# Expert sums of the second layer's sample rows built channel by channel, with their closing norm in that layout

## The chip, the cores and the metric

The kernel runs on one core of a Trainium2 chip. The metric is the device time of one execution in microseconds. Three runs of the kernel before gave 2985.22, 2985.74 and 2985.90 us, median 2985.74 us.

## The reference, cut to what matters

One inference step of a two-layer decoder: 512 prompt tokens and 8 sample tokens, 1024 channels, float32. Each layer has a mixer (attention and convolution in the first, pooling in the second) and then the part that fills most of the time, a retrieval of experts:

```python
def peer_ffn(h, wq, subkeys, u_tab, v_tab):
    ...
    expert = i1 * N_KEYS + i2                  # 16 of 16384 experts for each token and head
    g = jax.nn.softmax(cs, axis=-1)
    act = gelu(einsum('nd,nhkd->nhk', h, u_tab[expert]))
    return einsum('nhk,nhkd->nd', g * act, v_tab[expert])
...
xs = xs + peer_ffn(rms_norm(xs, norm_ffn[l]), ...)
y_prompt = rms_norm(xp, norm_final)
y_sample = rms_norm(xs, norm_final)
```

For each token and each of 8 heads, 16 experts are picked. Each brings a row u (1024 values, for a dot with the token) and a row v (1024 values, which is added with the weight of the dot). A closing RMS norm makes the two outputs y_prompt and y_sample.

## The kernel before

A **task** is one head of one tile of 128 prompt tokens: 16 steps, and in each step GpSimd gathers for each of the 128 tokens the pair (u, v) of one expert, 8 KB for each partition, 1 MB in all, into one of 8 slots of the buffer RING (line 935). A layer has 4 tiles of 8 heads, 32 tasks, and then one task for the 8 samples, in which the 128 partitions hold 64 (head, sample) pairs twice over, so that 8 steps (`PAIRS`) do for all of them. That sample task of the second layer is the last of the kernel, task 65.

What a step goes through, engine by engine:

- VectorE multiplies the u half of the slot with the token rows and sums it to a dot (`product`, line 2039; a row of one custom instruction and one read of the accumulator).
- ScalarE makes the gelu (L1500), the weight times it (`gate`, L1505) and a matrix `diag` (L1509): the identity times the weight for a prompt tile (128x128), the selector `sel_b` times it for the samples (128x8, which adds up the 16 partitions of each sample).
- TensorE multiplies (`accumulate`, line 1308): `diag` is the stationary operand, the v half of the slot the moving one, in two halves of 512 columns, into two PSUM banks. The sum of a tile stays in PSUM through its steps. Its end frees the slot (`v_freed`), for which GpSimd waits before it gathers the eighth step after.

In the trace a float32 matmul of the program shows as two records, each with its own weight load.

After the last step of a tile VectorE adds the sum to the rows X (`add_unit`, line 2070). The closing norm has three parts: `squares` (VectorE, lines 1566 and 1571), `root` (ScalarE, line 1410), `normed_rows` (VectorE, lines 1577 and 1585). The table `CLOSING` says at which step of which task they are issued; for the last prompt tile they are put into the sample task, `root` at step place 9 and `normed` at place 12 (in the sample task a step has two places: step 4 has places 8 and 9, step 6 has 12 and 13, step 7 has 14 and 15). For the samples they follow after everything else: `add_unit`, `squares`, `root`, `normed_rows`, then the store by the SP queue (line 727).

Beside the steps, the rest of the work of the next half-layer (projections, attention, pooling, query and key scores) is cut into **pieces**. `pieces` lists them with a weight each and `agenda` spreads them over the steps in proportion to the weights; each engine issues its part of a piece behind its part of that step. For the second half of the second layer the query pieces `q` lie between steps 704 and 816. `jobs_of` gives each piece its use of one of the PSUM banks that the pieces share in turn.

## Time and profile before

| | |
|---|---|
| median of 3 runs | 2985.74 us |
| the profiled execution | 2987.37 us, span of its trace 2985.4 us |
| granted TensorE clock, mean over the span | 0.972 |
| TensorE / VectorE / ScalarE / GpSimd busy | 87% / 70% / 43% / 41% |
| gathers by GpSimd | 1040 of 1 MB |
| mean rate of the DMA engines | 406 GB/s |
| the last gather | issued at 2959.33 us |

The trace's times are counted from the start of the span. The end of the span is the landing of the last store, y_sample. A granted clock of 1.00 is TensorE's upper level (2.4 GHz), 0.50 the lower (1.2 GHz); values between are means over a stretch in which it changed.

### The profile page before, as it was taken

The numbers are of one execution on the slowest core, as the hardware profiler recorded it, in microseconds if no ns is written. First come the engines' busy times: TensorE is split into PE (matmuls) and PEld (weight loads), VectorE is DVE, ScalarE is ACT, GpSimd is POOL, SyncE is SP. The second block draws the span as 40 slices with busy tenths as digits, with TensorE's granted clock in tenths as the row PEclk, the third lists the DMA queues.
The fourth block names the chain that finished last, engine by engine and source line by source line (L and its number), as shares of the span: only waits on it lengthen the run. The fifth ranks groups of instructions, "written<-read, shape, count | busy, mean of one in ns | idle before, by whom it ended". The sixth has DMA issues, their size and how long they took to land.

```text
span 2985.4 us, 26394 instructions
## 1 busy us (share of the span) xinstructions
PE 2590.8 (87%) x7285; PEld 1273.1 (43%) x7285; DVE 2076.5 (70%) x4938; ACT 1281.4 (43%) x3753; POOL 1220.2 (41%) x1104
## 2 busy tenths in 40 slices
PE   8999998999988888888888888888999978777787
PEld 6675564555544443334444334333444422222222
DVE  2657766887767667776667677777666766677666
ACT  2113445555434435444444444445443444444444
POOL 2013543444444434444444444445334444444442
PEclk9999999999999999999999999999999999999999
DMA  9979999999999999999999999999999999999997
GB/s 354 353 276 388 396 421 415 422 398 406 421 421 421 421 421 394 421 420 421 422 421 421 411 409 410 421 421 419 417 421 420 409 422 411 421 417 418 407 415 330
DMA packets 174565, 1213.29 MB, mean 406 GB/s; under 512 B 19685, under 2 KB 20721, under 8 KB 32843
## 3 DMA queue, kind: packets, MB, share of 16 engines
q0 software_dynamic: 155904, 1124.11, 91.5%
q1 hardware_dynamic: 18515, 87.51, 7.5%
q8 instruction: 58, 0.95, 0.1%
q14 instruction: 88, 0.72, 0.1%
HBM read 1206.90 MB, written 38.37 MB: 417 GB/s over the span
## 4 chain that ended last, share of the span: by engine, by line
DMA 45%; PE 36%; DVE 8%; ACT 6%; issue 3%; POOL 1%; ACTq 0%; POOLq 0%; DVEq 0%
DMA RING<-in_peer_uv,idx 44%; PE PSUM L1308 22%; PE PSUM L987 10%; DVE RING L2039 4%; ACT diag L1509 2%; ACT L1500 1%; PE PSUM L998 1%; ACT gate L1505 1%; DMA RING<-in_peer_uv,pidx 1%; POOL RING L935 1%; PE PSUM L969 1%; ACT act_h L1500 1%; ACT L1488 1%; PE PSUM L1296 1%; PE PSUM L1086 0%
## 5 line engine op out<-in xcount | busy, mean ns | idle before, releaser
L1308 PE MATMUL PSUM<-RING,diag 128*128 128x512 f32 (+1 forms) x4032 | 1957.3, 622 | 359.6 <-ACT diag L1509 353.3
L935 POOL DMA_INDIRECT RING<-in_peer_uv,idx x1024 | 1168.5, 1141 | 1550.3 <-PE PSUM L1308 1426.8
L2039 DVE CUSTOM_DVE_ANT_0 RING<-RING,H 128x1024 f32<-128x1024 f32 x1032 | 1262.3, 1224 | 703.3 <-DMA RING<-in_peer_uv,idx 697.5
L1308 PEld LDWEIGHTS PSUM<-RING,diag 128*128 128x128 f32 (+1 forms) x4032 | 731.5, 193 | 1425.7 <-ACT diag L1509 788.7
L1500 ACT ACTIVATE act_h<-dots 128x1 f32<-128x1 f32 x1040 | 208.1, 200 | 1108.7 <-DVE dots L2039 1107.1
L1509 ACT ACTIVATE diag<-ident,gate 128x128 f32<-128x128 f32 x992 | 398.3, 402 | 33.1 <-PE PSUM L1308 0.6
L987 PE MATMUL PSUM<-HT,WCH 128*128 128x256 f32 (+2 forms) x1408 | 334.0, 384 | 1.4 <-ACT HT L1361 1.3
L1505 ACT ACTIVATE gate<-act_h,ex 128x1 f32<-128x1 f32 x992 | 292.1, 294 | 32.3
L987 PEld LDWEIGHTS PSUM<-HT,WCH 128*128 128x128 f32 x1408 | 265.1, 192 | 93.6 <-issue 61.7
L1500 ACT ACT_TABLE_LOAD x90 | 115.5, 1283 | 5.6 <-DVE dots L2039 4.0
L1361 ACT ACTIVATE YT<-PSUM 128x256 f32<-128x256 f32 (+4 forms) x70 | 27.3, 390 | 173.9 <-PE PSUM L987 157.4
L2039 DVE DVE_READ_ACCUMULATOR2_ANT dots<- 128x1 f32 x1040 | 85.3, 82 | 0.0
L1488 ACT ACT_TABLE_LOAD x66 | 84.7, 1283 | 1.2
L1380 ACT ACTIVATE H<-H,negm 128x128 f32<-128x128 f32 (+3 forms) x32 | 18.0, 562 | 98.7 <-DVE negm L1741 98.6
L1296 PEld LDWEIGHTS PSUM<-SKT,YT 128*128 128x128 f32 (+1 forms) x316 | 41.4, 172 | 34.2 <-issue 29.9
L969 PE MATMUL PSUM<-ident,H 128*128 128x128 f32 (+1 forms) x200 | 33.9, 290 | 18.0 <-POOL POOL_STATE_M L884 9.7
L1296 PE MATMUL PSUM<-SKT,YT 128*128 128x128 f32 (+1 forms) x316 | 49.2, 278 | 0.0
L924 POOL DMA_DIRECT2D out_win_v_sample<-in_state_win_v x16 | 9.8, 617 | 92.9 <-PE PSUM L987 59.9
L987 PE MATMUL PSUM<-HT,RING 128*128 128x264 f32 x192 | 46.9, 402 | 0.0
L2017 DVE TENSOR_TENSOR onehot<-cij,iota 128x512 f32<-128x512 uint32 x65 | 44.6, 687 | 0.0
L2020 DVE TENSOR_TENSOR onehot<-onehot,si 128x512 f32<-128x512 f32 x65 | 44.6, 685 | 0.0
L2022 DVE TENSOR_REDUCE picked<-onehot 128x32 f32<-128x512 f32 x65 | 44.2, 680 | 0.0
(265 smaller groups left out, 1535.4 us busy)
## 6 DMA issues: line engine op xcount, KB each, us to landing
WCH<-in_peer_wq SPq DMA_DIRECT2D x28, 1024.0 KB, 9.1
WCH<-in_w_in_ab SPq DMA_DIRECT2D x18, 1024.0 KB, 9.6
RING<-in_peer_uv,idx POOLq DMA_INDIRECT x1024, 15.0
out_win_k_sample<-in_state_win_k POOLq DMA_DIRECT2D x8, 2016.0 KB, 12.0
out_win_v_sample<-in_state_win_v POOLq DMA_DIRECT2D x8, 2016.0 KB, 11.0
RING<-in_w_in_ab SPq DMA_DIRECT2D x6, 1024.0 KB, 11.8
WCH<-in_w_out_ab SPq DMA_DIRECT2D x6, 1024.0 KB, 9.6
X<-in_x_prompt SPq DMA_DIRECT2D x4, 512.0 KB, 4.4
```

The costliest lines, as they stand in the source:

```text
L935: pool.indirect_dma_start(rows[:, use % SLOTS, :], None, peer_uv.rearrange("l e n -> (l e) n"), bass.IndirectOffsetOnAxis(ap=at, axis=0),) ...
L969: last = nc.tensor.transpose(out[0:cols, n * width:n * width + rows], src, ident[0:rows, 0:rows])
L987: last = nc.tensor.matmul(out[:, lo:width], w[k], rows[:, k, lo:width], start=(k == 0), stop=(k == KD - 1))
L1296: last = nc.tensor.matmul(out[0:m, j * P:(j + 1) * P], qp[:, hc % 2, j * P:j * P + m], SKT[:, hc, :], start=True, stop=True)
L1308: last = nc.tensor.matmul(PSUM[0:out_n, accumulator(n) + half, :], diag[:, at % DIAGS, 0:out_n], rows[:, use % SLOTS, D + half * 512:D + h ...
L1488: nc.scalar.activation(ex[:, par, :], cs[:, par, :], ACT.Exp, bias=ncs[:, par:par + 1], accum_out=exsum[:, par:par + 1]).then_inc(gates_ex ...
L1500: chain(nc.scalar.activation(act_h[:, st, column], dots[:, st, column], ACT.Gelu))
L1505: chain(nc.scalar.activation(gate[:, st, column], act_h[:, st, column], ACT.Copy, scale=weight))
L1509: nc.scalar.activation(diag[:, at % DIAGS, 0:n], selector, ACT.Copy, scale=gate[:, st, column]).then_inc(diag_ready, 1)
L2017: left(V.tensor_tensor(onehot[:], cij[:].unsqueeze(3).to_broadcast([P, 2, TOP, TOP]), iota16[:].unsqueeze(1).unsqueeze(1).to_broadcast([P, ...
L2020: left(V.tensor_tensor(onehot[:], onehot[:], si[:].unsqueeze(2).to_broadcast([P, 2, TOP, TOP]), ALU.mult))
L2039: V.tensor_tensor_reduce(out=u, in0=u, in1=row, scale=1.0, scalar=0.0, op0=ALU.mult, op1=ALU.add, accum_out=dots[:, tau % SETS, k:k + 1]). ...
```

## The change

Three things are edited.

1. **The sum of the last task.** In the second layer's sample task `accumulate_turned` takes the place of `accumulate`. The roles of the operands are exchanged: the v half of the slot is the stationary operand, in 8 pieces of 128 channels, and `diag` (128x8) the moving one. So a step has 8 matmuls with 8 columns each in place of 2 with 512, and the sum stands with channels on the partitions: 128 x (8 pieces x 8 samples), in one PSUM bank. The residual is put in ahead of the first step by one matmul with the identity.
2. **The closing norm of the samples**, `last_unit`, in that layout: copy out of PSUM, square, a matmul with a matrix of 1/1024 that sums the squares over the partitions (`last_mean`), the product with the gains, a sum over the 8 pieces, root, reciprocal, product; all on 128x64 values or less. The store writes 128 rows of 64 values, and the host turns them round. For it the residual rows and the gains are needed in the new layout: a new piece `turned` (weight 1.5, at key column 8 of the queries of the last half-layer) has 16 small transposes on TensorE, two copies by ScalarE, and a memset by VectorE. The buffer is COUNT, which has no reader by then.
3. **The last tile's norm**: `normed` moves from place 12 to place 14 of the sample task, behind the dot of step 7. `root` stays at place 9.

```diff
-NORMS = (..., (1,), (2,), (3,), (4,), (0,))
+NORMS = (..., (1,), (2,), (3,), (4,))
...
+        if hc == 8 and (l, b) == (1, 1):
+            out.append((("turned",), 1.5))
...
-        found[task + 3 * (t == 0), 4 if t == 0 else 12] = [("normed", FINAL + t, 0)]
+        found[task + 3 * (t == 0), {0: 4, T - 1: 14}.get(t, 12)] = [("normed", FINAL + t, 0)]
...
-            sp.wait_ge(rows_normed, rows_by(FINAL + T))
-            store(y_sample.rearrange("b s d -> (b s) d"), Hv[0:B, 0, :])
+            sp.wait_ge(last_normed, 1)
+            store(y_sample, last_y)
...
+                if kind == "turned":
+                    pe.wait_ge(rows_normed, rows_by(FINAL - 1))
+                    for half in range(2):
+                        wait_emptied(pe, ("gain", FINAL, half))
+                    out = open_bank(piece)
+                    for c in range(KD):
+                        nc.tensor.transpose(out[:, c * B:(c + 1) * B], X[0:B, 0, c * P:(c + 1) * P], ident[0:B, 0:B])
+                    for c in range(KD):
+                        last = nc.tensor.transpose(out[:, KD * B + c:KD * B + c + 1], G[0:1, c * P:(c + 1) * P], ident[0:1, 0:1])
+                    close_bank(last, piece)
...
+            def accumulate_turned(n, tau, k):
+
+                use = first(tau) + k
+                at = tensor_rows(use)
+                out = PSUM[:, accumulator(n), 0:KD * B]
+                if k == 0:
+                    wait_emptied(pe, ("turned",))
+                    nc.tensor.matmul(out, ident[:], last_x, start=True, stop=False, skip_group_check=True)
+                pe.wait_ge(diag_ready, at + 1)
+                for c in range(KD):
+                    last = nc.tensor.matmul(out[:, c * B:(c + 1) * B], rows[:, use % SLOTS, D + c * P:D + (c + 1) * P],
+                                            diag[:, at % DIAGS, 0:B], start=False, stop=k == steps(tau) - 1,
+                                            skip_group_check=True)
+                last.then_inc(v_freed, 1)
+
+            def last_mean(n):
+
+                pe.wait_ge(mean_ready, 1)
+                pe.wait_ge(last_squared, 1)
+                nc.tensor.matmul(PSUM[:, accumulator(n) + 1, 0:KD * B], mean, last_square,
+                                 start=True, stop=True).then_inc(last_summed, 1)
...
-                    accumulate(n, sample_task(l), k, B, True, True)
+                    if l == L - 1:
+                        accumulate_turned(n, sample_task(l), k)
+                    else:
+                        accumulate(n, sample_task(l), k, B, True, True)
...
+                if kind == "turned":
+                    wait_full(act, piece)
+                    nc.scalar.activation(last_x, bank(piece)[:, 0:KD * B], ACT.Copy)
+                    emptied(nc.scalar.activation(last_g, bank(piece)[:, KD * B:KD * B + KD], ACT.Copy), piece)
...
-            front(("root", FINAL + T))
+            act.wait_ge(last_reduced, 1)
+            nc.scalar.activation(last_root, last_root, ACT.Sqrt, bias=eps[:, 0:1]).then_inc(last_rooted, 1)
...
+                dve.wait_ge(v_freed, tensor_rows(first(tau) + steps(tau)))
+                step(V.tensor_copy(last_y, total))
+                V.tensor_tensor(last_square, last_y, last_y, ALU.mult).then_inc(last_squared, 1)
+                wait_emptied(dve, ("turned",))
...
+                dve.wait_ge(last_summed, 1)
+                V.tensor_reduce(last_root, PSUM[:, accumulator(n) + 1, 0:KD * B].rearrange("p (c b) -> p b c", c=KD),
+                                AX.X, ALU.add).then_inc(last_reduced, 1)
+                dve.wait_ge(last_rooted, 1)
+                step(V.reciprocal(last_root, last_root))
...
-            add_unit(unit(1, T))
-            dve.wait_ge(acc_added, unit(1, T + 1))
-            squares(FINAL + T, 0)
-            normed_rows(FINAL + T, 0)
+            last_unit()
```

The first place is the end of TensorE's order. The last rows before (L1308 is the sum; 452 matmuls of the last prompt tiles, then the samples' 16):

```order
L1296 MATMUL PSUM<-SKT,YT 128x128 x2
L1296 MATMUL PSUM<-SKT,YT 8x128
L1308 MATMUL PSUM<-RING,diag 128x512 x452
L1308 MATMUL PSUM<-RING,diag 8x512 x16
L425 UNCONDITIONAL_BRANCH
```

And of the change (L1333 is the sum, L1346 to L1349 the new one, L1358 the mean of the squares):

```order
L1321 MATMUL PSUM<-SKT,YT 128x128 x2
L1321 MATMUL PSUM<-SKT,YT 8x128
L1333 MATMUL PSUM<-RING,diag 128x512 x452
L1346 MATMUL PSUM<-COUNT,ident 128x64
L1349 MATMUL PSUM<-diag,RING 128x8 x64
L1358 MATMUL PSUM<-COUNT 128x64
L429 UNCONDITIONAL_BRANCH
```

16 matmuls whose output is 8x512 have become 64 whose output is 128x8, with one ahead of them and one behind.

The second place is the end of VectorE's order. Before (L2039 is the dot, L1577 and L1585 the norm, L2070 the addition of the sum to X, L1566 and L1571 the squares):

```order
L2039 ISA dots 128x1
L1577 RECIPROCAL rstd<-rstd 128x5
L1585 SCALAR_TENSOR_TENSOR H<-X,rstd,G 128x1024
L2039 ISA RING,dots<-RING,KT 128x1024
L2039 ISA dots 128x1
L2070 TENSOR_TENSOR X<-PSUM,X 8x512 x2
L1566 ISA H,ss<-X 8x1024
L1566 ISA ss 8x1
L1571 TENSOR_SCALAR ss<-ss 128x5
L1577 RECIPROCAL rstd<-rstd 128x5
L1585 SCALAR_TENSOR_TENSOR H<-X,rstd,G 8x1024
```

Of the change (L2097 is the dot, L1633 and L1641 the norm of the last tile, L2138 and below `last_unit`):

```order
L2097 ISA RING,dots<-RING,KT 128x1024
L2097 ISA dots 128x1
L1633 RECIPROCAL rstd<-rstd 128x5
L1641 SCALAR_TENSOR_TENSOR H<-X,rstd,G 128x1024
L2138 COPY COUNT<-PSUM 128x64
L2139 TENSOR_TENSOR COUNT<-COUNT 128x64
L2141 TENSOR_TENSOR COUNT<-COUNT 128x64
L2144 TENSOR_REDUCE COUNT<-PSUM 128x8
L2147 RECIPROCAL COUNT<-COUNT 128x8
L2148 TENSOR_TENSOR COUNT<-COUNT 128x64
```

The norm of the last tile stands behind the last dot, and six instructions on 64 values or fewer for each partition have taken the place of six on 1024 or 512.

The third place is TensorE's order around the new piece, of the change (L1002 are query projections, L1321 key scores):

```order
L1321 MATMUL PSUM<-SKT,YT 128x128 x2
L1321 MATMUL PSUM<-SKT,YT 8x128
L1333 MATMUL PSUM<-RING,diag 128x512 x2
L1285 MATMUL PSUM<-ident,X 128x8 x8
L1287 MATMUL PSUM<-ident,G 128x1 x8
L1333 MATMUL PSUM<-RING,diag 128x512 x6
L1002 MATMUL PSUM<-HT,WCH 128x264 x4
```

The 16 transposes (L1285, L1287) stand in one lump between two steps; the query pieces after them lie up to 5 steps later than before, those ahead of them up to 3 steps earlier, and the last of them where they lay.

## Rows read from the trace of the kernel before

**Rows 1.** The page: shares of the chain that ended last, by engine.

```profile
DMA 45%; PE 36%; DVE 8%; ACT 6%; issue 3%; POOL 1%; ACTq 0%; POOLq 0%; DVEq 0%
```

**Rows 2.** Timeline of the last 30 us: start us, us, engine line op, xcount [idle before].

```profile
2959.74 1.88 PE L1308 MATMUL PSUM<-RING,diag 128*8 128x512 f32 x4 [0.69 <-ACT diag L1509]
...
2967.21 1.22 DVE L2039 CUSTOM_DVE_ANT_0 RING<-RING,KT 128x1024 f32<-128x1024 f32 x1 [1.25 <-DMA RING<-in_peer_uv,pidx]
...
2970.88 1.28 ACT L1500 ACT_TABLE_LOAD   x1
...
2972.04 1.22 DVE L2039 CUSTOM_DVE_ANT_0 RING<-RING,KT 128x1024 f32<-128x1024 f32 x1 [1.12 <-DMA RING<-in_peer_uv,pidx]
...
2973.09 5.58 PE L1308 MATMUL PSUM<-RING,diag 128*8 128x512 f32 x12 [1.81 <-ACT diag L1509]
...
2974.61 1.22 DVE L2039 CUSTOM_DVE_ANT_0 RING<-RING,KT 128x1024 f32<-128x1024 f32 x1
...
2976.44 0.30 ACT L1509 ACTIVATE diag<-sel_b,gate 128x8 f32<-128x8 f32 x1
...
2978.71 1.28 DVE L2070 TENSOR_TENSOR X<-PSUM,X 8x512 f32<-8x512 f32 x2 [2.87 <-PE PSUM L1308]
...
2981.48 0.21 ACT L1410 ACTIVATE rstd<-ss 128x5 f32<-128x5 f32 x1 [3.44 <-DVE ss L1571]
...
2983.25 0.30 SPq L727 DMA_DIRECT2D out_y_sample<-H  x1
```

**Rows 3.** DMA engines' GB/s in 40 slices of 0.1 us, 2972 to 2976 us.

```profile
GB/s 0 82 0 0 82 0 0 82 0 0 0 82 0 0 82 0 0 82 0 0 0 0 0 0 0 0 0 0 0 0 0 0 0 0 0 287 328 492 451 328
```

**Rows 4.** TensorE's timeline, behind an idle time (last row), and 16 narrow matmuls of the pooled samples.

```profile
1802.52 0.38 PE L1116 MATMUL PSUM<-POOL_NEW_M,H 8*128 8x8 f32 x2
...
1806.95 0.59 PE L1116 MATMUL PSUM<-POOL_NEW_M,H 8*128 8x8 f32 x2
...
2928.84 10.55 PE L1308 MATMUL PSUM<-RING,diag 128*128 128x512 f32 x20 [2.10 <-ACT diag L1509]
```

**Rows 5.** Stretches: us, busy PE, PEld, DVE, ACT, POOL, then granted clock, DMA share, GB/s.

```profile
1803.00:1804.00 1.00, 1.00 (x8) 0.94 (x8) 0.83 (x1) 0.00 (x0) 0.68 (x1) 1.00 1.04 434
1807.00:1808.00 1.00, 1.00 (x4) 0.94 (x4) 0.72 (x2) 0.39 (x3) 0.00 (x0) 0.50 1.06 442
...
161.50:162.00 0.50, 0.50 (x4) 0.47 (x3) 0.00 (x0) 0.00 (x0) 0.00 (x0) 0.74 0.97 406
162.00:162.50 0.50, 0.50 (x3) 0.47 (x3) 0.00 (x0) 0.00 (x0) 0.00 (x0) 0.50 1.10 406
...
2930.00:2931.00 1.00, 1.00 (x2) 0.33 (x1) 1.00 (x1) 0.00 (x0) 0.00 (x0) 0.50 1.08 451
```

**Rows 6.** Timeline, 8 narrow matmuls of the attention's samples.

```profile
159.94 0.38 PE L1046 MATMUL PSUM<-ident,RING 8*128 8x8 f32 x2
...
161.85 0.59 PE L1046 MATMUL PSUM<-ident,RING 8*128 8x8 f32 x2
...
162.37 0.59 PE L1047 MATMUL PSUM<-RING 64*128 64x8 f32 x2
162.99 0.19 DVE L1829 COPY YT<-PSUM 128x32 f32<-128x32 f32 x1 [3.69 <-PE PSUM L1047]
```

**Rows 7.** Timeline behind the pooled samples: a gather's issue and two dots.

```profile
1811.15 1.52 POOL L935 DMA_INDIRECT RING<-in_peer_uv,idx  x1 [7.47 <-PE PSUM L1308]
...
1818.03 1.24 DVE L2039 CUSTOM_DVE_ANT_0 RING<-RING,H 128x1024 f32<-128x1024 f32 x1 [0.63 <-DMA RING<-in_peer_uv,idx]
...
1820.83 1.23 DVE L2039 CUSTOM_DVE_ANT_0 RING<-RING,H 128x1024 f32<-128x1024 f32 x1 [0.95 <-DMA RING<-in_peer_uv,idx]
```

**Rows 8.** Stretches where the new piece will lie, and the end of the queries.

```profile
2260.00:2280.00 20.00, 19.63 (x62) 10.16 (x61) 13.41 (x30) 10.41 (x30) 8.81 (x9) 1.00 1.01 419
2375.00:2380.00 5.00, 5.00 (x16) 2.83 (x16) 3.92 (x14) 2.67 (x10) 3.06 (x3) 1.00 0.95 343
```

**Rows 9.** A small copy out of PSUM: ns min/median/max.

```profile
L1681 DVE COPY RING<-PSUM x1: 225/225/225, 31.6 to 31.6; 128x64 f32<-128x64 f32 x1
```

More of the change, by code:

```diff
@@ L81 @@
 TASKS = T * PH + 1
-NORMS = ((1, 2, 0), (1, 2, 0), (3, 4), (3, 4), (1, 2), (1, 2), (3, 4, 0), (3, 4, 0), (1,), (2,), (3,), (4,), (0,))
+NORMS = ((1, 2, 0), (1, 2, 0), (3, 4), (3, 4), (1, 2), (1, 2), (3, 4, 0), (3, 4, 0), (1,), (2,), (3,), (4,))
 FINAL = 8
@@ L371, in jobs_of @@
         return [(kind, piece[1], half) for half in range(2)]
+    if kind == "turned":
+        return [piece]
     if kind == "scored_sample":
@@ L496, in build @@
         rows = RING[:, :].rearrange("p (s n) -> p s n", n=ROW)
+        mean = COUNT[:, 0, :]
+        last_y, last_square = (COUNT[:, 1, n * KD * B:(n + 1) * KD * B] for n in range(2))
+        last_x = COUNT[:, 2, 0:KD * B]
+        last_g = COUNT[:, 2, KD * B:KD * B + KD]
+        last_root = COUNT[:, 2, KD * B + KD:KD * B + KD + B]
         hrep = (H[:, BT * D + D:BT * D + 2 * D], KT[:, :, :].rearrange("p c n -> p (c n)")[:, 0:D])
@@ L651, in build @@
         acc_added = sem("acc_added")
+        mean_ready = sem("mean_ready")
+        last_squared = sem("last_squared")
+        last_summed = sem("last_summed")
+        last_reduced = sem("last_reduced")
+        last_rooted = sem("last_rooted")
+        last_normed = sem("last_normed")
         def bank(name):
@@ L1344, in _ @@
                 for k in range(PAIRS):
-                    accumulate(n, sample_task(l), k, B, True, True)
+                    if l == L - 1:
+                        accumulate_turned(n, sample_task(l), k)
+                    else:
+                        accumulate(n, sample_task(l), k, B, True, True)
                     front_at(sample_task(l), k)
+            last_mean(unit(L - 1, T))
             assert len(opened) == len(JOBS)
@@ L1461, in front @@
                     copy_out(piece, pT_s[:, :, :], wide(piece, KD, B))
+                if kind == "turned":
+                    wait_full(act, piece)
+                    nc.scalar.activation(last_x, bank(piece)[:, 0:KD * B], ACT.Copy)
+                    emptied(nc.scalar.activation(last_g, bank(piece)[:, KD * B:KD * B + KD], ACT.Copy), piece)
                 if kind == "gain":
@@ L1912, in front @@
                     counted(*piece[1:])
+                if kind == "turned":
+                    V.memset(mean, 1.0 / D).then_inc(mean_ready, 1)
                 if kind == "qrep":
@@ L2073, in _, with last_unit @@
             NT = 2 * NK
+            def last_unit():
+                n, tau = unit(L - 1, T), sample_task(L - 1)
+                total = PSUM[:, accumulator(n), 0:KD * B]
+                dve.wait_ge(v_freed, tensor_rows(first(tau) + steps(tau)))
+                step(V.tensor_copy(last_y, total))
+                V.tensor_tensor(last_square, last_y, last_y, ALU.mult).then_inc(last_squared, 1)
+                wait_emptied(dve, ("turned",))
+                step(V.tensor_tensor(last_y.rearrange("p (c b) -> p c b", c=KD), last_y.rearrange("p (c b) -> p c b", c=KD),
+                                     last_g.unsqueeze(2).to_broadcast([P, KD, B]), ALU.mult))
+                dve.wait_ge(last_summed, 1)
[3 more added lines that the diff above has]
+                step(V.reciprocal(last_root, last_root))
+                V.tensor_tensor(last_y.rearrange("p (c b) -> p c b", c=KD), last_y.rearrange("p (c b) -> p c b", c=KD),
+                                last_root.unsqueeze(1).to_broadcast([P, KD, B]), ALU.mult).then_inc(last_normed, 1)
             def search_step(at):
@@ L2154 @@
         "norm_final"]
-_OUTS = [("y_prompt", (1, SEQ, D)), ("y_sample", (B, 1, D)), ("conv_prompt", (1, 1, 2, DA)),
+_OUTS = [("y_prompt", (1, SEQ, D)), ("y_sample", (P, KD * B)), ("conv_prompt", (1, 1, 2, DA)),
          ("conv_sample", (1, B, 2, DA)), ("win_k_prompt", (1, SEQ, DA)), ("win_k_sample", (1, B, PAST, DA)),
@@ L2187 @@
     out = {name: r.results[0][f"out_{name}"] for name, _ in _OUTS}
+    out["y_sample"] = _np.ascontiguousarray(out["y_sample"].reshape(P, KD, B).transpose(2, 1, 0)).reshape(B, 1, D)
     for name in ("win_k_prompt", "win_v_prompt"):
```

## The prediction

> **What bounds the kernel now.** I read the shares of the chain that ended last first [rows 1]: the landings of the gathers have 45% of it, TensorE 36%. That is the long middle, which the change touches in one place. The rest of the change lies in the last 26 us, so the timeline of that stretch decides [rows 2]. The reader is to see two halves in it. Until 2974.6 us VectorE waits for landings: step 3's dot starts at 2967.21 with 1.25 us of waiting and step 6's at 2972.04, also behind a wait, so a step lands every 2.4 to 2.5 us. Behind that stands a serial tail. The last `diag` is ready at 2976.74 (2976.44 + 0.30); TensorE works on steps 5, 6 and 7 without a pause from 2973.09 to 2978.67, 1.86 us a step. It is late there because ScalarE, which had made the last tile's root, had to load the gelu's table again at 2970.88. Then addition, squares, root and norm of the samples follow one another from 2978.71 to the store at 2983.25, 4.54 us, and 2.15 us later the span ends.
>
> **The change, part by part.**
>
> *The norm of the last tile.* It moves behind step 7's dot. Before, that dot began at 2974.61, behind the norm. When had its row landed? The DMA engines' slices show one 8 KB packet about every 0.33 us, the last at 2973.7 [rows 3], and step 6, whose row ended eight packets earlier, started its dot some 0.7 us behind its own last packet. So step 7 could have started at about 2974.45: the move gives 0.15 us, and only where TensorE is not behind. I take 0; the two ends are 0 and 0.15. The norm itself runs while TensorE sums, and its store, issued near 2977.2, lands long before the end.
>
> *The closing norm of the samples.* Removed are 4.54 us. Added behind TensorE's last matmul: a copy of 128x64 out of PSUM, 0.23 [rows 9]; a square, about 0.2 (nearest is the same row); the mean matmul with 64 columns, 0.4 at full clock (a narrow one alone takes 0.38 [rows 4]), 0.65 at half (0.59 [rows 6], and more columns); the sum over 8 pieces, the reciprocal and the last product, about 0.2 each (rows 9 again is nearest); the root, 0.21 [rows 2]; handovers between the engines, 0.03 to 0.05 each, 0.2. The gains' product lies beside the mean matmul. The sum is 1.85 us at full and 2.1 us at half clock, in place of 4.54: 2.4 to 2.7 us saved. The table for the root is loaded while TensorE still works, as before. The store moves the same 32 KB in 128 short pieces instead of 8 long ones; no row shows that price, I leave 2.15 us, with 0 and +0.5 as ends.
>
> *The sum of the last task.* A step becomes 8 matmuls with 8 moving columns and a new 128-column stationary operand each. The same shape is in the trace: in the pooled samples, 14 matmuls begin from 1802.52 to 1806.95, 0.316 us each [rows 4]. So a step costs 8 x 0.316 = 2.53 us instead of 1.86, 20.2 us for the task. The Trainium skill ("TensorE: Matmul & The Clock Gate", "LDWEIGHTS" and "Back-to-back issue gap") gives 107 ns for a load of 128 columns and 25 ns for a small matmul; from it I estimate 16 x 132 ns = 2.1 us a step, which would fit between two landings and take about 1.2 us off the full-clock sum below. The row goes first, and it says that TensorE is as slow as the landings already at full clock. At full clock, then: step 5's `diag` comes at 2973.05 as before, 24 matmuls follow, TensorE ends at 2973.09 + 7.58 = 2980.7 instead of 2978.7; + 1.85 + 2.15 = 2984.7. That alone is 0.7 us better than 2985.4.
>
> *But the clock will not stay.* Both places in the trace where TensorE does nothing but such narrow matmuls lose it. In the pooled samples it is 1.00 at 1803 and 0.50 from 1807 on, though TensorE was busy all the time [rows 5]; in the attention's samples, which start at 159.94, it falls within 161.5 to 162.0 and stands at 0.50 at 162.0 [rows 5, 6]. So the clock goes from its upper level (2.4 GHz) to its lower (1.2 GHz) 1.8 to 4.7 us into such a stream. It falls 40 times in the whole span; in all others TensorE had just stood idle, as the 2.10 us before 2928.84 and the 0.50 at 2930 show [rows 4, 5]. There the wide matmuls that follow bring it back; in the last task nothing wide follows. At the lower level the matmuls begin 0.52 us apart (161.85 to 162.37 [rows 6]), and VectorE gets the result at 162.99; I take 0.525. The 64 matmuls start at 2959.74 [rows 2]; the one ahead of them fits into TensorE's wait of 0.69 us there. With the fall 4.4 us in (nearer the second case, since here wide matmuls go before as there), 14 run at 0.316 (4.4 us) and 50 at 0.525 (26.3 us): TensorE ends at 2990.4, 11.8 us later than before. The landings are over by then; no `diag` is waited for any more (step 5's is ready at 2973.05, when TensorE would be at step 3). + 2.1 + 2.15 = 2994.7. The ends: a fall after 1.8 us, 2.0 us more; 0.45 to 0.60 for a matmul, 3.8 us to either side.
>
> *The piece `turned`.* 16 narrow matmuls, 16 x 0.316 = 5.1 us on TensorE at step 765, near 2270 us, with VectorE's memset and two copies by ScalarE of 0.2 us each, which nobody waits for. TensorE frees the slots of the ring, so this holds up the gathers. The pooled samples are the same lump: the next gather was issued after 7.47 us of waiting, and yet the dots slipped only from 2.48 to 2.80 us apart at one place [rows 7], 0.3 to 0.4 us in all, because eight slots were under way. At the new place TensorE is fuller, 19.63 of 20 us [rows 8]. I take 0.7 us. Upper end: nothing hidden, 5.1 + 1.7 for a fallen clock = 6.8; lower end: the pieces' shift removes the dip of 343 GB/s at 2375 [rows 8], which costs (421 - 343)/421 x 5 = 0.9 us.
>
> **The sum.** 2994.7 + 0.7 = 2995.4 against a span of 2985.4: +10.0 us. The profiled execution took 2987.37 us, so it would take 2997.4; it lies 1.6 us above the median of the runs, to which I add the same 10.0 (with rounding 10.1): **2995.8 us**, 0.34% slower. What a measurement of this kernel can tell from no change is 0.2%, 6.0 us.
>
> **The rivals.**
>
> *A: the clock stays up.* Then the span is 2984.7 + 0.7 = 2985.4, no change, 2985.7 us. The point from which it decides: every microsecond that the fall comes later is worth 0.66 us, and with no fall before 2979 there is nothing lost. For it speaks that TensorE would work without a gap from 2959.7 on, and 38 of 40 falls follow gaps; against it the two streams of rows 5 and 6, of which one was busy without a gap as well. The Trainium skill's rule is that the clock is lost where TensorE idles between bursts (the same page, "HAM oscillation — how this bites in real kernels"); by that rule a gapless stream keeps it and rival A holds. The trace disagrees at 1807. 14%.
>
> *B: TensorE at 0.5 is slower still.* If a narrow matmul doubles with the clock, 0.63, then 50 x 0.105 = 5.3 us more: 3001 us. Against: 161.85 to 162.37. 5%.
>
> *C: the lump hits the ring.* TensorE is over 90% busy there and the next pieces follow at once; if 3 to 5 us come through beside the forecast: 2999 to 3001 us. Against: rows 7. 7%.
>
> *D: the new sum costs nothing.* If a narrow step takes no more than the 1.86 us of a wide one and the clock stays, TensorE ends at 2978.7 as before, and 1.85 + 2.15 + 0.7 behind it make a span of 2983.4, 2983.7 us by the median. Against: rows 4. 3%.
>
> **How the numbers follow.** The forecast, a fall within 5 us and 0.5 to 0.56 a matmul, has 71%: 2992 to 2998. B and C lie above, A and D below. The range 2989.5 to 3000.5 holds the forecast, most of C and the lower end of the narrow matmuls' price; A, D and most of B are left out, just under 2 in 10. Slower by over 0.2% (above 2991.7): forecast, B, C, less 3% for a late fall or a cheap matmul, 0.80. Faster by over 0.2% (below 2979.8): no case reaches it, 0.01. Within: 0.19.
>
> **What would show it.** The granted clock at 0.50 from about 2964 us to the end; TensorE busy without a gap from 2959.7 to 2990; matmuls of L1349 0.32 us apart first, 0.52 later; VectorE's copy (L2138) waiting over 10 us for TensorE; from it to the store 2.1 us; the root's table loaded long before. Around 2270 us a wait of GpSimd for TensorE of 6 to 8 us, the clock at 0.50 for some microseconds, the dots late by under 1 us. The forecast is wrong if the clock stays at 1.00 in the last 20 us, if the last task's matmuls run in less than 0.25 us, or if the rows after 2300 us are shifted by more than 3 us against before.

## The result and the profile after

| | before | after |
|---|---|---|
| median of 22 runs each | 2985.43 us (2982.72 to 2989.22) | 2989.64 us (2985.62 to 2994.12) |
| profiled execution | 2987.37 us | 2986.24 us |
| its span | 2985.4 us | 2984.3 us |
| mean granted clock of TensorE | 0.972 | 0.966 |

The ratio is 1.0014, 95% interval 1.0008 to 1.0020: the change costs 4.2 us. That is real and small, under the 0.2% (6.0 us) that the prediction called no change. The forecast was 2995.8 us, 10.1 us more: the sign and the mechanism were right, the size was more than twice what came, and the result lies only 0.1 us inside the lower end of the range (2989.5). That it lies inside is luck, since the interval of the ratio alone spans 2.4 to 6.0 us over the kernel before. The class on which I put 0.80, slower by over 0.2%, did not come.

The profiled execution of after is shorter than that of before, though its median is longer. The middle ends some microseconds earlier or later from run to run (here the last task starts at 2954.53, before at 2959.74 [rows 2]), so spans of single executions don't compare. What compares is **the tail**: from TensorE's first matmul of the last task to the end of the span. Before it is 2985.4 - 2959.74 = 25.7 us, after 2984.3 - 2954.53 = 29.8 us: +4.1 us, as much as the medians differ. The medians leave nothing for the middle, within the 2 us either way that their interval leaves open; the trace of the middle, below, shows no loss there either.

TensorE's timeline of the changed kernel's end (start us, us, engine line op, xcount in matmul records, of which a float32 matmul makes two, and the idle time before):

```profile
2951.95 1.98 PE L1333 MATMUL PSUM<-RING,diag 128*128 128x512 f32 x4 [0.50 <-ACT diag L1564]
2953.77 0.33 PE L1346 MATMUL PSUM<-COUNT,ident 128*128 128x64 f32 x2
2954.53 1.95 PE L1349 MATMUL PSUM<-diag,RING 128*128 128x8 f32 x16 [0.43 <-ACT diag L1564]
2956.82 2.26 PE L1349 MATMUL PSUM<-diag,RING 128*128 128x8 f32 x16 [0.34 <-ACT diag L1564]
2959.29 20.65 PE L1349 MATMUL PSUM<-diag,RING 128*128 128x8 f32 x96 [0.21 <-ACT diag L1564]
2980.61 0.66 PE L1358 MATMUL PSUM<-COUNT 128*128 128x64 f32 x2 [0.67 <-DVE COUNT L2139]
```

Step 0 takes 1.95 us and TensorE then waits for the next `diag`: at full clock a narrow step is hardly dearer than a wide one (1.88 [rows 2]), and the landings set the pace as before. Step 1 already takes 2.26. From step 2 on six steps run without a gap in 20.65 us, 3.44 us each, and TensorE is the bound. The stretches say why (us, busy PE, PEld, DVE, ACT, POOL, granted clock, DMA share, GB/s):

```profile
2956.00:2958.00 2.00, 1.67 (x16) 1.57 (x15) 1.96 (x3) 0.70 (x3) 0.00 (x0) 1.00 1.01 422
2958.00:2959.00 1.00, 1.00 (x7) 0.98 (x7) 0.34 (x2) 0.56 (x3) 0.00 (x0) 0.65 1.05 434
...
2960.00:2970.00 10.00, 10.00 (x49) 10.00 (x49) 6.27 (x12) 5.97 (x15) 0.00 (x0) 0.50 0.37 155
2970.00:2979.00 9.00, 9.00 (x44) 9.00 (x44) 2.10 (x4) 2.08 (x4) 0.00 (x0) 0.50 0.14 58
```

The granted clock falls in the stretch 2958 to 2959; 0.65 there is 30% at 1.00 and 70% at 0.50, so at about 2958.3, 3.8 us into the narrow stream. It stands at 0.50 (1.2 GHz) to the end, with TensorE busy all the time.

The other engines at the end (same columns; lines not of TensorE left in):

```profile
2967.02 1.22 DVE L2097 CUSTOM_DVE_ANT_0 RING<-RING,KT 128x1024 f32<-128x1024 f32 x1 [1.21 <-DMA RING<-in_peer_uv,pidx]
...
2969.48 1.23 DVE L2097 CUSTOM_DVE_ANT_0 RING<-RING,KT 128x1024 f32<-128x1024 f32 x1 [1.23 <-DMA RING<-in_peer_uv,pidx]
...
2979.98 0.23 DVE L2138 COPY COUNT<-PSUM 128x64 f32<-128x64 f32 x1 [7.84 <-PE PSUM L1349]
...
2981.37 0.23 DVE L2144 TENSOR_REDUCE COUNT<-PSUM 128x8 f32<-128x64 f32 x1 [0.78 <-PE PSUM L1358]
2981.63 0.30 ACT L1588 ACTIVATE COUNT<-COUNT,eps 128x8 f32<-128x8 f32 x1 [8.72 <-DVE COUNT L2144]
...
2982.45 0.33 SPq L742 DMA_DIRECT2D out_y_sample<-COUNT  x1
```

Step 7's dot (2969.48) waits for its landing, 2.46 us behind step 6's: with the norm out of the way VectorE is at the landings' pace. It did not matter, since TensorE began step 7 only near 2976.5 (one step of 3.44 us before its end), 5 us behind the `diag` of that step (made at 2971.61). VectorE waits 7.84 us for TensorE's last sum. From its copy to the store's issue are 2.47 us instead of 4.54 (2978.71 to 2983.25 [rows 2]), from the issue to the end 1.85 instead of 2.15.

The piece `turned`, in the middle, from TensorE's part of the timeline:

```profile
2255.15 0.65 PE L1285 MATMUL PSUM<-ident,X 8*128 8x8 f32 x8
...
2255.67 0.63 PE L1287 MATMUL PSUM<-ident,G 1*128 1x1 f32 x8
...
2256.22 1.98 PE L1333 MATMUL PSUM<-RING,diag 128*128 128x512 f32 x4
```

16 transposes are 16 records, not 32: a float32 transpose shows as one record here, a float32 matmul as two. The lump takes 1.07 us (2255.15 to 2256.22), and the clock stays at 1.00 there. VectorE's dots around it start at 2253.24, 2255.72, 2258.26 and 2260.70, still 2.4 to 2.5 us apart, and GpSimd's waits for TensorE next to it are 1.45 and 2.05 us. So two signs that the prediction gave did not come, a wait of GpSimd of 6 to 8 us and some microseconds at 0.50.

### The profile page after: what moved, and what is told of

The parts are those of the page before. It is cut to its first block, busy times and chain, and to the rows that moved or that the text cites. A ratio compares the mean times of both kernels' runs of the same rounds, so it can differ in the third digit from the quotient of the medians.

```text
span 2984.3 us, 26630 instructions
## 1 busy us (share of the span) xinstructions
PE 2599.8 (87%) x7401; PEld 1298.7 (44%) x7401; DVE 2073.6 (69%) x4938; ACT 1281.4 (43%) x3755; POOL 1233.7 (41%) x1104
## 4 chain that ended last, share of the span: by engine, by line
DMA 46%; PE 36%; DVE 8%; ACT 7%; issue 3%; POOL 1%; ACTq 0%; POOLq 0%; DVEq 0%
DMA RING<-in_peer_uv,idx 44%; PE PSUM L1333 21%; PE PSUM L1002 9%; DVE RING L2097 4%; ACT diag L1564 2%; ACT L1555 1%; ACT gate L1560 1%; DMA RING<-in_peer_uv,pidx 1%; PE PSUM L1013 1%; ACT act_h L1555 1%; PE PSUM L984 1%; PE PSUM L1349 1%; ACT L1543 1%; POOL RING L950 1%; PE PSUM L1321 1%
## 5 line engine op out<-in xcount | busy, mean ns | idle before, releaser
L1333 PE MATMUL PSUM<-RING,diag 128*128 128x512 f32 x4000 | 1940.1, 622 | 351.3 <-ACT diag L1564 345.6
L950 POOL DMA_INDIRECT RING<-in_peer_uv,idx x1024 | 1183.6, 1156 | 1532.5 <-PE PSUM L1333 1401.7
L2097 DVE CUSTOM_DVE_ANT_0 RING<-RING,H 128x1024 f32<-128x1024 f32 x1032 | 1262.6, 1224 | 695.6 <-DMA RING<-in_peer_uv,idx 689.5
L1333 PEld LDWEIGHTS PSUM<-RING,diag 128*128 128x128 f32 x4000 | 730.2, 194 | 1398.4 <-ACT diag L1564 766.1
L1002 PE MATMUL PSUM<-HT,WCH 128*128 128x256 f32 (+2 forms) x1408 | 334.2, 384 | 1.6 <-ACT HT L1412 1.4
L1002 PEld LDWEIGHTS PSUM<-HT,WCH 128*128 128x128 f32 x1408 | 265.4, 192 | 94.1 <-issue 62.1
L2097 DVE DVE_READ_ACCUMULATOR2_ANT dots<- 128x1 f32 x1040 | 85.9, 83 | 0.0
L1321 PEld LDWEIGHTS PSUM<-SKT,YT 128*128 128x128 f32 (+1 forms) x316 | 42.0, 174 | 34.5 <-issue 30.2
L1321 PE MATMUL PSUM<-SKT,YT 128*128 128x128 f32 (+1 forms) x316 | 49.7, 280 | 0.0
L1002 PE MATMUL PSUM<-HT,RING 128*128 128x264 f32 x192 | 46.9, 402 | 0.0
## 6 DMA issues: line engine op xcount, KB each, us to landing
RING<-in_w_in_ab SPq DMA_DIRECT2D x6, 1024.0 KB, 11.7
```

Of the source, the lines that this page charges most:

```text
L950: pool.indirect_dma_start(rows[:, use % SLOTS, :], None, peer_uv.rearrange("l e n -> (l e) n"), bass.IndirectOffsetOnAxis(ap=at, axis=0),) ...
L1002: last = nc.tensor.matmul(out[:, lo:width], w[k], rows[:, k, lo:width], start=(k == 0), stop=(k == KD - 1))
L1321: last = nc.tensor.matmul(out[0:m, j * P:(j + 1) * P], qp[:, hc % 2, j * P:j * P + m], SKT[:, hc, :], start=True, stop=True)
L1333: last = nc.tensor.matmul(PSUM[0:out_n, accumulator(n) + half, :], diag[:, at % DIAGS, 0:out_n], rows[:, use % SLOTS, D + half * 512:D + h ...
L2097: V.tensor_tensor_reduce(out=u, in0=u, in1=row, scale=1.0, scalar=0.0, op0=ALU.mult, op1=ALU.add, accum_out=dots[:, tau % SETS, k:k + 1]). ...
```

## The experiments

Ten kernels, two of them measured a second time, in four sets; each set had its own runs of the kernel before on its own chip, with medians of 2985.13, 2985.69, 2986.72 and 2984.89 us. A ratio is always to the kernel before of the same set. Tails are taken as above, in each kernel's own profile.

### The moved norm alone

The kernel before with this one edit:

```diff
-        found[task + 3 * (t == 0), 4 if t == 0 else 12] = [("normed", FINAL + t, 0)]
+        found[task + 3 * (t == 0), {0: 4, T - 1: 14}.get(t, 12)] = [("normed", FINAL + t, 0)]
```

> The kernel before with the last tile's norm moved behind the last dot, and nothing else. All theories: step 7's dot follows step 6's landing by 2.4 us instead of 2.57, TensorE is the one that is late there anyway, so from the first matmul of the sample task to the end of the span 25.6 us as before (25.66), 25.5 at best; the median within 1 us of before.

Measured: 2985.25 us (10 runs) against 2985.13, ratio 1.0002 (0.9992 to 1.0011); the tail is 2983.5 - 2957.87 = 25.6 us. Its timeline:

```profile
2971.22 5.55 PE L1308 MATMUL PSUM<-RING,diag 128*8 128x512 f32 x12 [1.81 <-ACT diag L1509]
...
2972.70 1.23 DVE L2039 CUSTOM_DVE_ANT_0 RING<-RING,KT 128x1024 f32<-128x1024 f32 x1 [1.23 <-DMA RING<-in_peer_uv,pidx]
...
2976.80 1.28 DVE L2070 TENSOR_TENSOR X<-PSUM,X 8x512 f32<-8x512 f32 x2 [1.45 <-PE PSUM L1308]
```

The last dot now starts behind a landing instead of behind the norm, and TensorE still ends with three steps in a row, 5.55 us behind the late `diag` of step 5: TensorE was behind already, for the reason given in the prediction (the table load), and an earlier last `diag` is worth nothing.

### All eight steps wide, only the closing new

The changed kernel with the last sum as before (rows by 8), then 8 transposes behind the last step, the residual's add and the new closing. Core of the edit:

```diff
-                    if l == L - 1:
+                    if l == L - 1 and k >= WIDE:
                         accumulate_turned(n, sample_task(l), k)
...
+            turn_part()
             last_mean(unit(L - 1, T))
```

with `WIDE = 8`; `turn_part` transposes `part_rows`, into which ScalarE and VectorE copy the two halves of the sum.

> All 8 steps summed in the old layout, the sum turned at the end by two half copies and 8 transposes, closing norm in the new layout. Both theories: TensorE's sum ends 18.9 us after the first matmul of the task as before, copies 0.65, transposes 0.7, closing 2.2, store 1.9 us: 24.4 us, 1.3 us below before; this is what the new closing norm is worth alone, less the turn. If the new closing norm were no gain, 26 us or more.

Measured: 2984.25 us (10 runs), ratio 0.9996 (0.9986 to 1.0006); tail 2982.6 - 2958.13 = 24.5 us.

```profile
2971.47 5.53 PE L1339 MATMUL PSUM<-RING,diag 128*8 128x512 f32 x12 [1.81 <-ACT diag L1583]
...
2977.04 0.68 DVE L2159 COPY H<-PSUM 8x512 f32<-8x512 f32 x1 [1.45 <-PE PSUM L1339]
...
2977.87 0.63 PE L1368 MATMUL PSUM<-ident,H 8*128 8x8 f32 x8 [0.86 <-DVE H L2159]
...
2979.12 0.41 PE L1376 MATMUL PSUM<-COUNT 128*128 128x64 f32 x2 [0.62 <-issue]
...
2980.71 0.33 SPq L748 DMA_DIRECT2D out_y_sample<-COUNT  x1
```

So the new closing gains 1.2 us even when the turn is paid for at the end, and with the clock up its mean matmul takes 0.41 us, not 0.66. This kernel also contains the piece `turned`: the median is 0.9 us under that of before, where the tail alone gives 1.2. That fits a middle that costs nothing, but ten runs can't tell it closer than 3 us (the interval).

### How many narrow steps

The same code with other values of `WIDE`: steps from `WIDE` on are narrow, the wide part of the sum is turned behind the first narrow step, and VectorE adds it. (Here ScalarE makes the last tile's root two places earlier too.)

> Steps 0 to 5 of the last task summed in the old layout, their sum copied out and turned by 8 transposes while steps 6 and 7 are summed in the new one; closing norm in the new layout; squares and root of the last tile one step earlier. Theory clock: only two steps are narrow and end before the clock can fall, so TensorE ends 18.8 us after its first matmul of the task and the span 22.8 us after it, 3 us below before. Theory shape: the two steps cost 3.4 us each: 26 us, as before.

> Steps 0 to 6 of the last sum wide as before the change, only step 7 narrow, the sum of the seven turned by 8 transposes behind step 7, then the new closing. With six wide steps the tail was 23.7 us (median 2982.9 us), with all eight wide 24.5 us. If narrow steps cost by the clock alone, the clock stays at 1.00 through the closing here: step 7 1.9 us, transposes 0.65, mean matmul 0.41 instead of 0.66; the tail is 23.4 us and the median 2982.5 us. If turning behind a narrow step loses the clock all the same, 23.8 us, median 2983.

> Steps 0 to 3 of the last sum wide, 4 to 7 narrow, the turn behind step 4, then the new closing: between six wide (tail 23.7 us) and none (29.8). The first narrow matmul comes behind the table load, near 2967.1 us on the clock of the six-wide profile. If the clock falls about 4 us into the narrow stretch, steps 4 and 5 and the transposes take 4.7 us, steps 6 and 7 3.44 us each at half clock, TensorE ends near 2978.7 and the tail is 26.8 us. If the clock stays at 1.00 over a stretch this short, TensorE ends near 2975.7 and the tail is 23.4 us.

| narrow steps | kernel | median (runs) | ratio to before | tail |
|---|---|---|---|---|
| 0 | eight wide | 2984.25 (10) | 0.9996 (0.9986 to 1.0006) | 24.5 us |
| 1 | seven wide | 2983.20 (10) | 0.9990 (0.9980 to 0.9999) | 24.4 us |
| 2 | six wide | 2982.90 (10) | 0.9991 (0.9981 to 1.0001) | 23.7 us |
| 4 | four wide | 2987.17 (1) | | 28.2 us |
| 8 | the change | 2989.64 (22) | 1.0014 (1.0008 to 1.0020) | 29.8 us |

The jump lies between two and four; three were not run. The kernel with one narrow step is the only one whose interval stays below 1, by a hair. With two narrow steps, in the first of their two profiles, the first runs at 1.00, and the fall comes only in the last half microsecond of the sum (2975.2 of 2975.7):

```profile
2970.99 1.90 PE L1357 MATMUL PSUM<-diag,RING 128*128 128x8 f32 x16
...
2972.82 0.66 PE L1369 MATMUL PSUM<-ident,H 8*128 8x8 f32 x8
...
2973.59 2.12 PE L1357 MATMUL PSUM<-diag,RING 128*128 128x8 f32 x16
...
2976.34 0.66 PE L1377 MATMUL PSUM<-COUNT 128*128 128x64 f32 x2 [0.62 <-issue]
```

The expectation for two was 22.8 us, and 23.7 came. TensorE ended 19.4 us behind its first matmul of the task instead of 18.8, since step 7 had to wait for its `diag` until 2973.59, and the mean matmul ran at half clock (0.66 us, not 0.41).

With four, the clock falls at about 2970.0, 2.2 us into the narrow stretch, and the last three steps take 3.47 us each:

```profile
2967.81 1.95 PE L1357 MATMUL PSUM<-diag,RING 128*128 128x8 f32 x16 [1.45 <-ACT diag L1583]
2969.69 0.85 PE L1369 MATMUL PSUM<-ident,H 8*128 8x8 f32 x8
2970.47 10.41 PE L1357 MATMUL PSUM<-diag,RING 128*128 128x8 f32 x48
```

I had expected 26.8 us there with a fall 4 us in; it came 1.8 us sooner, and the tail was 28.2. With one narrow step both expectations were missed, 23.4 and 23.8, where 24.4 came: the clock fell 2.2 us in, so that most of the transposes ran at half, 0.81 us instead of 0.66. They stand behind the last step there: between the end of that step (2975.30) and VectorE's addition (2976.41) lie 1.1 us of turning and copying that nothing hides.

### Does wide work hold the clock?

The forecast says that the narrow stream itself, not an idle gap, loses the clock. Then wide matmuls put between the narrow steps, though useless, could shorten the whole. Each kernel is the changed one with a filler ahead of steps 1 to 7 (the constants' one before the wait for `diag`, the others behind it), into the spare bank, where its result is never read. The core of the four edits:

```diff
 # constants, one of 512 columns
+                    nc.tensor.matmul(PSUM[:, accumulator(n) + 1, 0:FILL], ident[:],
+                                     POOL_CUR[:, :, :].rearrange("p g n -> p (g n)")[:, 0:FILL], start=True, stop=True)
 # half of the wide step before the change
+                    nc.tensor.matmul(PSUM[0:B, accumulator(n) + 1, 0:512], diag[:, at % DIAGS, 0:B],
+                                     rows[:, use % SLOTS, D:D + 512], start=True, stop=True)
 # the row's half with 128 columns of weights
+                    nc.tensor.matmul(PSUM[:, accumulator(n) + 1, 0:512], ident[:],
+                                     rows[:, use % SLOTS, D:D + 512], start=True, stop=True)
 # the whole wide step: both halves
+                    for half in range(2):
+                        nc.tensor.matmul(PSUM[0:B, accumulator(n) + 1, 0:512], diag[:, at % DIAGS, 0:B],
+                                         rows[:, use % SLOTS, D + half * 512:D + half * 512 + 512], start=True, stop=True)
```

> The changed kernel with one wide matmul (512 columns, identity times a constant, into a bank that nobody reads) ahead of each of the steps 1 to 7 of the last task. Theory clock: the narrow steps are dear only because the granted clock falls; the wide matmuls hold it at 1.00, a narrow step takes 1.9 us and a filler 0.86, TensorE ends 21.5 us after its first matmul of the task, and the span 25.5 us after it (the changed kernel: 29.8), about 4 us less in the median. Theory shape: narrow steps cost 3.4 us whatever the clock, so with fillers 4.3 us and more: 36 us to the end, 6 us slower than the changed kernel.

> The changed kernel with a wide matmul ahead of steps 1 to 7 that is one half of the wide step before the change: the same diagonal of 8 columns as weights, the same 512 columns of the gathered row moving, into the spare bank, its result never read. The constants' filler did not hold the clock: it fell 4.5 us in and the tail took 40.9 us. Theory 'data' (what the operands hold counts, constants that are mostly zeros do not): the granted clock stays at 1.00 to the end, a step takes 0.93 + 1.95 = 2.9 us, TensorE ends 0.4 + 1.95 + 7 x 2.9 = 22.7 us behind its first matmul of the task, and with 1.9 + 1.9 behind it the tail (from the first matmul of the task to the span's end) is 26.5 us. Theory 'share' (a stream that is narrow by half loses the clock whatever the wide part holds): the clock falls 4 to 5 us in, a step takes 2.0 + 3.4 = 5.4 us less what 8 columns of weights save, and the tail is 40 to 42 us, as with the constants.

> As the kernel with the half of a wide step as filler, but with the identity of 128 columns as weights: 512 columns of the gathered row moving. It tells the weights from the moving data. If what moves decides, it goes as that kernel does whichever way that is (26.5 us if held, 41 if not). If the constant weights were at fault, the clock falls here and the tail is 40 to 42 us while it is held there.

> As the kernel with the half of a wide step ahead of steps 1 to 7, but with both halves: a whole wide step of real data in the spare bank ahead of each narrow one, so that half of TensorE's time is wide at either clock. If narrow matmuls only dilute the stream and this share of wide work is enough, the clock holds at 1.00: steps of 1.86 + 1.95 = 3.8 us, TensorE ends 0.4 + 1.95 + 7 x 3.8 = 29 us behind its first matmul of the task and the tail is 33 us. If a stretch of 2 us of narrow matmuls loses it whatever stands between the stretches, the clock falls at the second or third of them; then it either comes back in each wide part (steps of 4 to 6 us) or stays at 0.50: steps of 3.7 + 3.4 = 7.1 us, tail 54 us.

| filler before each of steps 1 to 7 | median (runs) | tail | clock |
|---|---|---|---|
| none (the change) | 2989.64 (22) | 29.8 us | 0.50 from 3.8 us in |
| one, constants | 2999.56 (4) | 40.9 us | 0.50 from 3.2 us in |
| one, real row, 8 columns of weights | 3001.80 (2) | 44.0 us | 0.50 from 2.1 us in |
| one, real row, 128 columns of weights | 3000.56 (1) | 41.7 us | 0.50 from 3.3 us in |
| two, real row | 2991.24 (1) | 32.3 us | 1.00 through the sum |

With one filler the clock falls as without, and a narrow step goes from 1.95 to over 3.4 us. No filler of the three kept it up, whatever it held, so nothing speaks for my idea that zeros and constants were at fault. The constants' tail of 40.9 us met neither expectation (25.5 and 36): I had not reckoned with fillers at half clock, 1.85 us each. The kernel with one half of the wide step:

```profile
2956.79 1.95 PE L1353 MATMUL PSUM<-diag,RING 128*128 128x8 f32 x16 [0.43 <-ACT diag L1568]
2959.08 1.88 PE L1350 MATMUL PSUM<-RING,diag 128*8 128x512 f32 x2 [0.34 <-ACT diag L1568]
2960.89 3.58 PE L1353 MATMUL PSUM<-diag,RING 128*128 128x8 f32 x16
...
2992.81 3.58 PE L1353 MATMUL PSUM<-diag,RING 128*128 128x8 f32 x16
```

Here the clock had gone at about 2958.9 (1.00 in 2958.0 to 2958.5, 0.86 in 2958.5 to 2959.0, then 0.50), 0.2 us before the first filler began. So this profile doesn't show a filler failing to hold the clock, only fillers failing to bring it back; with the other two fillers it fell at about 2960.2, behind the first filler or at its very end. The kernel with both halves, and two of its stretches:

```profile
2961.09 1.95 PE L1354 MATMUL PSUM<-diag,RING 128*128 128x8 f32 x16
2962.97 1.88 PE L1351 MATMUL PSUM<-RING,diag 128*8 128x512 f32 x4
...
2983.26 1.95 PE L1354 MATMUL PSUM<-diag,RING 128*128 128x8 f32 x16
2985.87 0.41 PE L1363 MATMUL PSUM<-COUNT 128*128 128x64 f32 x2 [0.67 <-DVE COUNT L2144]
```

```profile
2970.00:2975.00 5.00, 5.00 (x27) 2.75 (x27) 3.28 (x6) 2.90 (x9) 0.00 (x0) 1.00 0.02 7
...
2980.00:2985.00 5.00, 5.00 (x34) 3.44 (x33) 0.00 (x0) 0.00 (x0) 0.00 (x0) 1.00 0.00 0
```

Twice the useless work (14 wide matmuls instead of 7) makes the tail 11.7 us shorter, and all eight narrow steps take 1.95 us. The same narrow matmuls, with the same operands and banks, take 1.95 us a step at 1.00 and 3.4 to 3.6 at 0.50: this shows that the clock is what makes them dear. Whether the second wide half is what held it is less sure: up to the first filler both kernels do the same, and one had lost the clock by then, the other had not. Was it luck in one run? The same kernel again, in more:

> The same kernel as e9_hold_two, for more than one run: it held the clock at 1.00 with a tail of 32.3 us and took 2991.24 us, where half as much wide work in the same places lost the clock and took 3001.8. If holding is what this much wide work does every time, all runs lie within 2989 to 2994 us. If it was luck of where the fall would have come, some runs lie 20 us higher, near 3012 us.

Measured: 2994.02 us, eight runs: 2992.36, 2991.96, 2996.85, 3008.92, 2992.55, 2994.77, 3001.94, 2993.27; ratio 1.0038 (1.0021 to 1.0055). Its profile again shows 1.00 through the whole sum. Only four of the eight lie within the 2989 to 2994 us expected of a clock that is always held, and none near the 3012 of one that isn't. Two lie 8 and 15 us above the median, where those of the kernel before spread over 5 us in that set. The run of 3008.92 us has the lowest mean clock of the eight, 0.965, which fits a loss for part of the sum; that of 3001.94 has 0.971, like the others (0.970 to 0.974). They have no trace, so what happened in them isn't shown. Over all runs seven of nine with two fillers took 2991 to 2997 us, and all seven with one filler 2999 to 3003: the wide work holds the clock mostly, not surely.

### The row that priced a narrow matmul

My 0.316 us came from the pooled samples [rows 4], where matmuls over 120 rows and over 8 rows alternate. Here the eight with 120 rows go first, then the eight with 8 rows. (The pooled samples' sums are started and added to in another order and are not computed as before; count and shapes are the same.)

```diff
                 for ch in range(KD):
...
                     nc.tensor.matmul(o_, pstate[0:B * PS, ch * P:(ch + 1) * P], POOL_STATE_M[0:B * PS, g, :],
-                                     start=True, stop=False)
+                                     start=True, stop=False, skip_group_check=True)
+                for ch in range(KD):
+                    g = ch * P // GW
+                    o_ = out[:, ch * B:(ch + 1) * B]
                     last = nc.tensor.matmul(o_, Hv[0:B, 0, ch * P:(ch + 1) * P], POOL_NEW_M[0:B, g, :],
```

> The kernel before, only the pooled samples' 16 narrow matmuls written in another order: first the 8 with 120 rows, then the 8 with 8 rows. The forecast's 0.316 us for a narrow matmul came from them in alternating order; the last sum's narrow matmuls took 0.24 at full clock. If the change between 120 and 8 rows is what made that row dear, all 16 now begin 0.23 to 0.25 us apart at full clock. If the small operands themselves or their partition count are, the 8 with 8 rows stay at 0.3 us or more, and the 8 with 120 rows go at 0.24. If neither, 0.316 for all 16.

```profile
1800.18 1.85 PE L1114 MATMUL PSUM<-POOL_STATE_M,HT 120*128 120x8 f32 x16
1801.96 1.95 PE L1119 MATMUL PSUM<-POOL_NEW_M,H 8*128 8x8 f32 x16
1803.84 8.40 PE L1311 MATMUL PSUM<-RING,diag 128*128 128x512 f32 x15
```

Both groups run at 0.23 to 0.24 us a matmul, (1803.84 - 1800.18) / 16 = 0.23. In the old order each matmul cost 0.08 us more; neither the few rows nor the shape did. The new order changes two things at once: the row count no longer alternates, and two matmuls in a row no longer add into the same 8 columns. The alternation is the likelier cause, since the two records of every narrow matmul of the last sum go into the same columns too and are only 0.12 us apart; the two were not tested one by one. A second thing is in its stretches:

```profile
1804.00:1805.00 1.00, 1.00 (x3) 0.51 (x4) 1.00 (x4) 0.94 (x5) 0.00 (x0) 1.00 1.01 418
1805.00:1806.00 1.00, 1.00 (x2) 0.29 (x1) 0.59 (x2) 0.81 (x4) 0.00 (x0) 0.63 1.02 426
1806.00:1807.00 1.00, 1.00 (x3) 0.45 (x2) 1.00 (x1) 0.00 (x0) 0.48 (x1) 0.50 1.08 451
```

The clock falls at about 1805.3, when the narrow matmuls have been over for 1.4 us and wide ones are running: the price of a narrow stretch can fall on the work behind it.

### Six wide steps and two narrow, again

Six wide steps and two narrow had the shortest tail; it ran again in more rounds.

> The kernel with steps 0 to 5 wide and 6 and 7 narrow again, in five rounds: it had the shortest tail of all, 23.7 us against 25.7 before the change and 29.8 with it, and a median of 2982.9 us in ten runs against 2985.1. If the tail is all that differs, the median is again 2.0 to 2.3 us under that of before, ratio 0.9993, and the two sets together tell it from no change; if the first set was luck, the ratio is 0.9998 to 1.0002.

Measured: 2984.97 us (11 runs) against 2986.72, ratio 0.9996 (0.9987 to 1.0005); its tail 2979.8 - 2956.24 = 23.6 us. The ratio falls between the two expectations (0.9993, or 0.9998 to 1.0002). Both sets lie under before, by 2.2 and 1.8 us, and both profiles show a tail 2.0 to 2.1 us shorter; each interval alone reaches 1, so that it beats the kernel before is likely but not proven. Against the change it is clear: both intervals end below 1.0006, that of the change begins at 1.0008.

One thing the tail doesn't contain: in every run of the other kernels the device time is 1.9 to 2.0 us longer than the span, but in 7 of the 21 runs with six wide steps it is 2.2 to 3.0 us longer, 2.8 in the second profile. By the spans the two medians are 2.4 and 2.5 us under before, by the device times 2.2 and 1.8. So part of what the tail gains is lost behind the end of the span in a third of the runs; nothing here shows to what.

## Why the prediction came out as it did

**Right: the clock.** The forecast's main step, that the last task's narrow stream loses the clock although TensorE is never idle for long, held in its place and nearly in its time: 3.8 us in, where I took 4.4 and gave 1.8 to 4.7 as the ends. In the other kernels that lost it in the last sum or its transposes, it fell 2.1 to 4.2 us in, inside the same ends. The Trainium skill's rule that the clock is lost at idle gaps between bursts ("TensorE: Matmul & The Clock Gate", "HAM oscillation — how this bites in real kernels") is not what happened here: when it fell at 2958.3 TensorE had been idle for at most 0.43 us at a time since 2953.77, and 2960 to 2979 us is all busy and all at 0.50. Rival A, which rested on that rule, fell.

**Wrong: the price of a narrow matmul, at both clocks.** I took 0.316 us at full and 0.525 at half. Measured are 1.95 / 8 = 0.24 and 3.44 / 8 = 0.43. The step that failed is the sentence "The same shape is in the trace": the sequence was not the same, since in rows 4 the row count alternates between 120 and 8. The grouped pooled samples show that the order made the price. The half-clock row [rows 6] alternates as well, between 8 rows (L1046) and 64 (L1047), and at full clock its matmuls stand 0.31 to 0.32 us apart like the pooled ones (160.25, 160.57, 160.88); it too gave a price that the new stream did not pay. There was a nearer estimate in the text, the one I worked out from the Trainium skill ("TensorE: Matmul & The Clock Gate", "LDWEIGHTS" and "Back-to-back issue gap"), 2.1 us a step at full clock; measured was 1.95. I set it aside for the row. One of the prediction's own signs of being wrong came with this, a matmul of the last task in less than 0.25 us. The consequence was that I had TensorE at the landings' pace already at full clock (2.53 against 2.4 to 2.5 us), when it has half a microsecond to spare. (A smaller slip: a fall after 1.8 us instead of 4.4 costs 2.6 x 0.66 = 1.7 us in that reckoning, not 2.0.)

**The sum, term by term:**

| term | predicted | measured | difference |
|---|---|---|---|
| TensorE, first matmul of the last task to the end of the last | 14 x 0.316 + 50 x 0.525 = 30.7 us | 2979.94 - 2954.53 = 25.4 us | -5.3 |
| closing, to the store's issue | 2.1 | 2980.0 to 2982.45, with the handover 2.5 | +0.4 |
| store to the end | 2.15 | 1.85 | -0.3 |
| `turned` in the middle | +0.7 | none to be seen, taken as 0 | -0.7 |
| moved norm | 0 | 0 | 0 |

Together -5.9 us, and 10.1 - 5.9 = 4.2 us. The last tenths of this agreement are chance, as the medians are not known so closely.

**The closing** was right in kind (4.54 predicted to fall to 2.1, measured 2.47) and a little short: its operations took 2.07 us instead of 1.9 (the root 0.30 instead of 0.21), and the handovers between them 0.4 us instead of 0.2. The store was expected to cost 0 to 0.5 us more in 128 short pieces; it took 0.3 us less, in every kernel that has it (1.8 to 1.9 us from issue to the end of the span, against 2.15 and 2.16 in the two profiles with the old form).

**`turned`** was mis-sized by a factor of five, 5.1 us instead of 1.07: the narrow row's price again, and I priced a transpose like a matmul, which has two records where a transpose has one. That cost little in the sum, since I took 0.7 us of it to come through.

**The moved norm** was right, at 0 with TensorE behind.

**Rival D** (a narrow step costs nothing and the clock stays) had 3% and was half true: the narrow step costs 1.95. Had the clock stayed up, TensorE would have ended one narrow step behind the last `diag`, near 2973.8, and with 2.2 and 1.85 us behind it the tail would have been some 23.3 us, 2.4 under before. So the change's idea was sound by that much, and the clock took over 6 us back. This is worked out from the timeline, not run; the kernel with two narrow steps came to 23.6.

## What to carry to other kernels

Before a sum is turned so that its large operand becomes the weights and a few columns move, ask how long TensorE would then do nothing else. Here the clock was halved with every number of narrow steps that was run, with TensorE busy or nearly so. With one or two narrow steps it fell so late that it cost some tenths; with four or eight it cost more, on the path that sets the end, than the shorter closing saves. Turn only the last steps of the sum.

When a row of another place prices new work, compare the sequence around it too, not only the instruction's shape: narrow matmuls whose row counts alternated cost a third more here. And compare ends by a tail measured from a fixed event, where single runs of one kernel spread over 6 us and more, and set the device times beside it, for what lies behind the span.

## What the runs showed of the hardware

- Useless wide work can pay for itself: 14 extra matmuls of 0.93 us left the tail at 32.3 us, 7 of them at 44.0 us (two of nine runs with the 14 took 8 and 15 us more than the median).
- The clock fell 1.4 us after the last of 16 narrow matmuls, in the wide ones that followed.
- A float32 transpose of 8x128 is one record, 8 of them 0.63 to 0.66 us at full clock (0.08 each); a narrow float32 matmul is two of 0.12 us each.
- Writing 32 KB out in 128 short pieces took 0.3 us less from issue to end than in 8 long ones.
